# Residual sums by transposes in PSUM, the norm factor after the FFN products, and gate loads queued after weights

## The reference

```
h = rms_norm(x) ; p = h @ w_in
A = gated delta rule(p)   ; B = forgetting attention(p)
y = sigmoid(gA) * (A @ w_branch_a) + sigmoid(gB) * (B @ w_branch_b)
x = x + y @ w_out
x = x + (silu(n @ w_gate) * (n @ w_up)) @ w_down   with n = rms_norm(x)
out = rms_norm(x)         # each norm with its own gain vector
```

## Time and profile before

| what | us |
|---|---|
| device time, median of 3 runs | 1346.81 (1346.26 to 1347.42) |
| profiled execution, span first to last instruction | 1345.4 |
| PE busy | 1274.8 (95%) |
| DVE, ACT, POOL busy | 516.1, 470.4, 465.6 |
| mean granted TensorE clock | 0.971 of full |

### The profile page before, as it was taken

The page is one execution under the profiler, slowest core; times in us unless marked ns, Lnnn a source line. Parts: engine busy times, 40 slices in busy tenths (PEclk is TensorE's granted clock), DMA queues, the critical chain, the costliest instruction groups (busy, mean ns, idle before and its releaser), DMA issues.

```text
span 1345.4 us, 18394 instructions
## 1 busy us (share of the span) xinstructions
PE 1274.8 (95%) x6571; PEld 1062.1 (79%) x6571; DVE 516.1 (38%) x890; ACT 470.4 (35%) x890; POOL 465.6 (35%) x229
## 2 busy tenths in 40 slices
PE   5999979989899899999999998999799999999996
PEld 4868869879789798888888886878588888878884
DVE  4334452342342422466666674441333333330003
ACT  5344462433533523444444432323322222221113
POOL 5334440320411402333333322443344444444442
PEclk9999989998998999999999998999899999999998
DMA  6323320210211302433232206443133333332321
GB/s 168 81 71 94 99 73 25 71 48 24 80 44 44 94 25 70 118 89 87 87 87 86 86 16 217 134 118 94 36 104 95 94 94 95 103 115 85 92 73 63
DMA packets 172452, 113.66 MB, mean 84 GB/s; under 512 B 6257, under 2 KB 157922, under 8 KB 172402
## 3 DMA queue, kind: packets, MB, share of 16 engines
q1 hardware_dynamic: 166034, 98.26, 25.8%
q10 hardware_dynamic: 6368, 14.72, 3.0%
HBM read 104.54 MB, written 8.42 MB: 84 GB/s over the span
## 4 chain that ended last, share of the span: by engine, by line
PE 41%; issue 17%; POOL 5%; DVE 1%; ACT 1%; POOLq 0%; DVEq 0%; ACTq 0%
PE ps L1150 28%; PE ps L1494 9%; POOL w_lo L493 5%; PE ps L1238 2%; PE ps L1132 1%; POOL rstd L488 0%; DVE xn L1103 0%; ACT raw L564 0%; DVE Tm L946 0%; DVE h_lo L846 0%; DVE mixT L1124 0%; ACT tmp L803 0%; DVE Tm L949 0%; DVE L L944 0%; DVEq L64 0%
## 5 line engine op out<-in xcount | busy, mean ns | idle before, releaser
L493 POOL TENSOR_TENSOR w_lo<-raw,w_hi 128x1024 fp32r<-128x1024 f32 x170 | 415.4, 2444 | 791.9 <-ACT w_hi L554 791.9
L1150 PE MATMUL ps<-h_hi,w_lo 128*128 128x512 f32 x992 | 407.8, 411 | 0.0
L1150 PE MATMUL ps<-h_hi,w_hi 128*128 128x512 f32 x992 | 391.5, 395 | 4.7 <-DVE h_lo L846 2.6
L1150 PE MATMUL ps<-h_lo,w_hi 128*128 128x512 f32 x992 | 393.1, 396 | 0.0
L554 ACT ACTIVATE w_hi<-raw 128x1024 fp32r<-128x1024 f32 x170 | 180.4, 1061 | 577.3 <-PE ps L1150 480.4
L1150 PEld LDWEIGHTS ps<-h_lo,w_hi 128*128 128x128 f32 x992 | 187.1, 189 | 38.9 <-issue 1.0
L1150 PEld LDWEIGHTS ps<-h_hi,w_hi 128*128 128x128 f32 x992 | 187.9, 189 | 36.7 <-DVE h_lo L846 3.1
L1150 PEld LDWEIGHTS ps<-h_hi,w_lo 128*128 128x128 f32 x992 | 189.5, 191 | 32.0 <-issue 1.0
L867 DVE SCALAR_TENSOR_TENSOR tmp<-ps,prm,tmp 128x511 f32<-128x511 f32 (+2 forms) x72 | 53.9, 749 | 92.3 <-ACT tmp L591 87.1
L1113 DVE TENSOR_TENSOR tmp<-gate,ps 128x512 f32<-128x512 f32 x22 | 15.1, 688 | 154.1 <-PE ps L1150 154.1
L820 DVE TENSOR_TENSOR f_lo<-tmp,f_hi 128x512 f32 x22 | 58.9, 2675 | 2.7
(11 more groups left out here) (228 smaller groups left out, 1662.3 us busy)
## 6 DMA issues: line engine op xcount, KB each, us to landing
raw<-in_w_in SPq DMA_DIRECT2D x80, 512.0 KB, 3.9
raw<-in_w_gate SPq DMA_DIRECT2D x22, 512.0 KB, 3.8
raw<-in_w_up SPq DMA_DIRECT2D x22, 512.0 KB, 3.8
raw<-in_w_down SPq DMA_DIRECT2D x22, 512.0 KB, 3.8
gate_dram<-gate ACTq DMA_DIRECT2D x24, 256.0 KB, 2.0
cumb<-cum_dram ACTq DMA_DIRECT2D x8, 512.0 KB, 3.6
raw<-in_w_branch_a SPq DMA_DIRECT2D x8, 512.0 KB, 6.0
raw<-in_w_branch_b SPq DMA_DIRECT2D x8, 512.0 KB, 3.7
```

The source lines that it names most:

```text
L493: pool.tensor_tensor(w_lo[:, r % 2, :], raw[:, r, :], w_hi[:, r % 2, :], ALU.subtract)\
L1150: return pe.matmul(ps[:, bank, :], wts[wl][k], acts[xl][:, k, :], start=(n == 0), stop=(n == len(PASSES) - 1))
```

## The change

- **Layout.** `half_neg` becomes 32 floats, `prm` 128 floats, the small per-row tiles 32 floats each: all multiples of 128 bytes.
- **SP.** Weight loads of group i+1 are issued ahead of the gate loads of group i. ACT's `branches` is as before.
- **OUT.** PE adds the residual to the bank of the unit by four transposes without clearing (`residual`). ACT and DVE take `h_hi`, `h_lo` from the sum with the gain alone; DVE also copies it to `x2T`. PE turns `x2T` to token-major banks 4 to 7 only for the row sums.
- **FFN.** The factor is spread to a 128x512 tile `rstdb` by one matmul on a diagonal tile (`wide_row`). DVE multiplies both products by it, ACT applies Silu in place and makes `f_hi`.
- **Down.** f is stationary and the weights move, one k-tile to a load, so the sum is token-major. x2T is added by transposes during k = 1. The last k-tile goes row block by row block.

```diff
+    LINE = 32
-        half_neg = keep("half_neg", [P, 2 * H])
-        prm = keep("prm", [P, NPRM])
+        half_neg = keep("half_neg", [P, LINE])
+        prm = keep("prm", [P, P])
-        ss = keep("ss", [P, 2 * TT])
+        ss = keep("ss", [P, LINE])
...
@@ block.sync
-            with sp.Fori(0, KT // 2) as i:
+            def load_ab(i):
                 for r in range(4):
                     load(i + AB0, r, col_tile(w_branch_b if r >= 2 else w_branch_a,
                                               (i + AB0) * (2 * P) + (r % 2 - 2 * AB0) * P))
+            def load_gates(i):
                 for r in range(2):
-                    sp.wait_ge(b_low, led(b_low, FH // 2))
                     sp.wait_ge(y_sum, led(y_sum, i * 2 + r - 1))
                     sp.dma_start(gin[:, r, :, :], gate_dram[1:3, bass.ds(i * 2 + r, 1)]
                                  .rearrange("k j p n -> p (k j) n")).then_inc(gin_loaded[r], 16)
+            def load_out(i):
+                for r in range(4):
+                    load(i + OUT0, r, col_tile(w_out, i * (4 * P) + r * P))
+            load_ab(0)
+            load_ab(1)
+            sp.wait_ge(b_low, led(b_low, FH // 2))
+            load_gates(0)
+            with sp.Fori(1, KT // 2 - 1) as i:
+                load_ab(i + 1)
+                load_gates(i)
+            load_out(0)
+            load_gates(KT // 2 - 1)
+            load_out(1)
...
@@ block.gpsimd
+            for r in range(3):
+                low_part(FFN0, r)
+            pool.wait_ge(ms_ready, TT + 1)
+            power(rstd[:, 0:TT], ms[:, 0:TT], TT).then_inc(rstd_ready, 1)
+            low_part(FFN0, 3)
...
@@ block.scalar
+            def half_squares(a):
+                act.wait_ge(x2_turned, 4 * a + 4)
+                for t in range(TT):
+                    act.activation(gin[:, t // 2, t % 2, :], ps[:, 4 + t, :], ACT.Square,
+                                   accum_out=ss[:, a * TT + t:a * TT + t + 1]).then_inc(sq_summed, 1)
+            for j in range(KT):
+                high_ahead(OUT0 + j // 4, j % 4)
+                act.wait_ge(unit_done, OUT0 * 4 + j + 1)
+                act.activation(h_hi[:, j, :], ps[:, j % 4, :], ACT.Copy,
+                               scale=prm[:, NFFN + j:NFFN + j + 1]).then_inc(h_high, 1)
+                if j == 4:
+                    half_squares(0)
+            half_squares(1)
+            def ffn(i, first=False):
+                high_ahead(i + FFN0, 0)
+                if first:
+                    act.wait_ge(wide_done, 1)
+                    act.activation(rstdb[:, :], ps[:, 4, :], ACT.Copy).then_inc(wide_ready, 1)
+                silu(i, 0)
+                if not first:
+                    f_high(i - 1, 1)
+                high_ahead(i + FFN0, 1)
+                high_ahead(i + FFN0, 2)
+                silu(i, 1)
+                f_high(i, 0)
+                high_ahead(i + FFN0, 3)
...
+            for t in range(TT):
+                act.wait_ge(down_done, t + 1)
+                act.activation(raw[:, t, :], ps[:, 2 * t:2 * t + 2, :].rearrange("p b n -> p (b n)"),
+                               ACT.Square, accum_out=ss[:, 2 * TT + t:2 * TT + t + 1]).then_inc(sq_summed, 1)
@@ block.vector
+                    if kept:
+                        copy(x2T[:, k, :], ps[:, k % 4, :]).then_inc(x2_copied, 1)
...
+            def ffn_pair(i, k, first=False):
+                j = i * 2 + k
+                dve.wait_ge(unit_done, (i + FFN0) * 4 + 2 * k + 1)
+                dve.tensor_tensor(gate[:, k, :], ps[:, 2 * k, :], rstdb[:, :], ALU.mult)\
+                    .then_inc(ffn_scaled, 1)
+...
+                dve.wait_ge(unit_done, (i + FFN0) * 4 + 2 * k + 2)
+                dve.tensor_tensor(tmp[:, k, :], ps[:, 2 * k + 1, :], rstdb[:, :], ALU.mult)\
+                    .then_inc(ffn_up, 1)
+                dve.wait_ge(ffn_gate, led(ffn_gate, j + 1))
+                dve.tensor_tensor(tmp[:, k, :], tmp[:, k, :], gate[:, k, :], ALU.mult).then_inc(ffn_mul, 1)
...
@@ block.tensor
+            def x2_turn(j):
+                def go():
+                    pe.wait_ge(x2_copied, j + 1)
+                    if j == 4:
+                        pe.wait_ge(sq_summed, 2 * TT)
+                    for t in range(TT):
+                        last = turn(ps[:, 4 + t, j % 4 * P:(j % 4 + 1) * P], x2T[:, j, t * P:(t + 1) * P])
+                    last.then_inc(x2_turned, 1)
+                return go
+            for j in range(KT):
+                if j >= 4:
+                    pe.wait_ge(h_low, KT + j - 3)
+                    pe.wait_ge(x2_copied, j - 3)
+                unit(OUT0 + j // 4, j % 4, y_hi, y_lo, [x2_turn(j - 1), residual(j)] if j else [residual(j)],
+                     None if j else (y_low, led(y_low, KT)))
+            def ffn(i, first=False):
+                for r in range(4):
...
+                    tasks = ([x2_turn(KT - 1)], [], [wide_row], [])[r] if first else ()
+                    unit(i + FFN0, r, h_hi, h_lo, tasks, (h_low, 2 * KT) if first and r == 0 else None)
+            def down(k):
...
+                if k == FT - 1:
+                    order = [(t, n, p) for t in range(TT) for p in range(3) for n in range(2)]
+                else:
+                    order = [(t, n, p) for p in range(3) for t in (2, 3, 0, 1) for n in range(2)]
+                for at, (t, n, p) in enumerate(order):
...
+                    last = pe.matmul(ps[:, 2 * t + n, :], xt[:, k, t * P:(t + 1) * P],
+                                     wt[:, r % 2, n * 512:n * 512 + 512], start=(k == 0 and p == 0),
+                                     stop=(k == FT - 1 and p == 2))
```

More of the change, by code:

```diff
@@ L558, in high_ahead, with norm_high @@
                 high_part(q if r < 2 else q + 1, (r + 2) % 4)
[L560 to L567, removed]
+            def norm_high(col):
                 for k in range(KT):
-                    act.wait_ge(x_turned, KT * n + k + 1)
+                    act.wait_ge(x_turned, k + 1)
                     act.activation(h_hi[:, k, :], ps[:, k % 4, :], ACT.Copy,
@@ L779, in _ @@
-            act.wait_ge(out_added, led(out_added, KT))
-            half_squares(1, x_res, lambda t: xn2[:, t, D // 2:])
-            norm_high(1, NFFN)
-            def ffn(i):
-                for r in range(4):
-                    high_ahead(i + FFN0, r)
-                    if r % 2 == 0:
-                        act.wait_ge(unit_done, (i + FFN0) * 4 + r + 1)
-                        act.wait_ge(ffn_mul, led(ffn_mul, i * 2 + r // 2 - 1))
-                        act.activation(gate[:, r // 2, :], ps[:, r, :], ACT.Silu).then_inc(ffn_gate, 1)
@@ L1442, in _, with add_turned @@
                     unit(i + AB0, r, b_hi if r >= 2 else a_hi, b_lo if r >= 2 else a_lo)
-            def out_group(i):
-                def back_turn(r):
-                    def go():
-                        pe.wait_ge(out_taken, led(out_taken, i * 4 + r + 1))
-                        pe.wait_ge(out_added, led(out_added, i * 4 + r - 1))
-                        for t in range(TT):
-                            last = turn(ps[:, 4 + r % 2, t * P:(t + 1) * P], back[:, r % 2, t * P:(t + 1) * P])
-                        last.then_inc(out_turned, 1)
-                    return go
-                for r in range(4):
-                    pe.wait_ge(out_taken, led(out_taken, i * 4 + r - 3))
-                    unit(i + OUT0, r, y_hi, y_lo, [back_turn(r - 1)] if i or r else [],
-                         None if i or r else (y_low, led(y_low, KT)))
-                if i == KT // 4 - 1:
-                    back_turn(3)()
+            def add_turned(bank, col, src, stop=False):
+                return pe.matmul(ps[:, bank, col:col + P], src, ident[:, :], start=False, stop=stop,
+                                 is_transpose=True)
@@ new lines, in wide_row @@
+            def wide_row():
+                pe.wait_ge(diag_ready, 1)
+                pe.matmul(ps[:, 4, :], step[:, 4 * P:5 * P], tmp[:, 0, :], start=True, stop=True)\
+                    .then_inc(wide_done, 1)
+            def ffn(i, first=False):
+                for r in range(4):
+                    if not first:
+                        s = ffn_up if r % 2 else ffn_scaled
+                        pe.wait_ge(s, led(s, i * 2 + r // 2 - 1))
+                    tasks = ([x2_turn(KT - 1)], [], [wide_row], [])[r] if first else ()
+                    unit(i + FFN0, r, h_hi, h_lo, tasks, (h_low, 2 * KT) if first and r == 0 else None)
@@ L1475, in _ @@
             pe.wait_ge(h_low, 2 * KT - 1)
[L1476 removed]
+            pe.wait_ge(x2_copied, KT - 1)
+            ffn(0, True)
             with pe.Fori(1, FT // 2) as i:
                 ffn(i)
[L1481 to L1500 removed]
@@ L1516 @@
+            pe.wait_ge(ffn_scaled, led(ffn_scaled, FT))
+            pe.wait_ge(ffn_low, led(ffn_low, FT - 2))
+            for k in range(FT):
+                if k == FT - 2:
+                    pe.wait_ge(ffn_low, led(ffn_low, FT))
+                down(k)
```

272 lines of the change are left out of this document (121 added, 151 removed).

## The result

The changed kernel takes 1358.94 us (median of 4 runs, 1354.71 to 1359.85); beside it the kernel before took 1346.53 (4 runs). The ratio is 1.0089, interval 1.0072 to 1.0105: 0.9% slower, clear of noise. The forecast was 1353 with a range of 1340 to 1362, slower: direction and range held, the size was half of what came (+6.2 forecast; +12.4 between the medians, +12.7 between the two profiled spans, 1345.4 and 1358.1).

The account below looks back on a forecast made before the run. PE, busy for 95% of the span, was taken as the bound. Terms 20.3 - 4.3 + 8.0 - 7.1 - 0.95 - 2.3 - 7.4 = +6.2 took 1345.4 to 1351.6, with 1.4 for the median 1353; range 1340 to 1362.

Parts of the forecast that it names:

- AB: AB: gate loads behind weights make PE stand 4.5 us, plus 2.2 of half clock, for groups 1 to 3; +20.3 us.
- The 1.0 for `y_lo`: End of AB's group 3: late gate products on DVE let OUT begin some 1.0 us after the weights.
- OUT: OUT: PE stands 0.7 us ahead of the 12th matmul in seven units, more after the squares; +8.0 us, 56.4 against 48.4.
- OUT to FFN and FFN: OUT to FFN 9.9 us instead of 17.0, with a 5.9 stop (-7.1); FFN hides vector work, stop before down goes (-0.95).
- Layout: All stages: with lines of 128 bytes, matmuls moving 512 columns take 0.227 us everywhere; small matmuls in delta rule and attention -4.3.
- the forecast's own sign of being wrong: Wrong if sigmoids in groups 1 to 3 do not wait for DMA, or matmuls on a and y stay at 0.234.
- Start: Delta rule and attention, ahead of AB: 1216 + 320 small matmuls 3 ns cheaper each by layout; -4.3 us.
- Down and tail: Down 123.4 us against 125.7, -2.3; tail after the last matmul 7.7 us against 15.1, -7.4.
- Gates in time: Rival, AB: gates reach ACT by T1 + 6.7, no stops, AB -9.0 instead of +20.3, time 1324; chance 0.12.
- Full clock: Rival, AB and FFN: the four new stops leave the clock up, 8.8 us less, 1344; chance 0.14.
- The clock falls in OUT: Rival, OUT: standing and transposes drop the clock, 192 matmuls cost 40 us more, 1388; chance 0.03.
- FFN no longer hides: Rival, FFN: DVE holds POOL 2.7 us in each second unit, 15 us more, 1368; chance 0.05.

Follow-up runs that it names:

- experiment 1: The kernel before with only SP's new order, next group's weight loads ahead of the gate loads: 1366.01 us, 1.0152 of before.
- experiment 2: The changed kernel with SP's old order of loads in AB and OUT: 1338.82 us, 0.995 of the kernel before.
- experiment 7: Changed kernel, SP's old order, OUT's x2T turn ahead of the 16th matmul, ACT rounding in the first FFN group without waiting for the wide row: 1323.13 us, 0.985.
- experiment 9: On experiment 7: group 0's gates ahead of half of group 1's weights, its sigmoids later, and staged tiles a multiple of 2048 bytes from h_hi: 1312.52 us, 0.9768.
- 4: The kernel before with y_hi and y_lo lying in the place of h_hi and h_lo: 1339.79 us, one run, no interval.
- Experiment 3: The kernel before with only the small tiles' sizes changed, so every tile starts on a whole line of 128 bytes: 1343.32 us, 0.9984.
- experiment 5: The kernel before with h_hi and h_lo declared behind the small tiles: 1355.98 us, 1.0077.
- 11: On experiment 9: four small attention tiles moved behind b_lo, so a and b also start at a multiple of 2048 bytes: 1312.33 us, 0.9751.

## Why the prediction was right, and where its size was off

- **AB, +18.2 for +20.3: right in mechanism and place.** The last weight load at T1 + 3.6, the gates right behind it, rounding behind the sigmoids, POOL last: every link is in the timeline, and experiment 1 shows it alone. Each stop was 0.8 less than the 4.5 taken, because the three loads took 6.7 us (844.5 to 851.2) and not 7.5. The 1.0 for `y_lo` was too small: the stop ahead of OUT is 7.50, 3.8 more than the others, of which the forecast had 1.0. I had charged one operation stretched by POOL; it was two, since POOL ran two subtractions in a row. The half clock was booked in AB for all three stops (6.6); that behind the last one fell into OUT, and this alone makes AB some 2.4 too dear in the forecast and OUT as much too cheap.
- **OUT, +12.3 for +8.0: the stops right, the size 4.3 short.** Of it 2.4 came from outside, that half clock behind the 7.50 (experiment 2 against the changed kernel). The four turns behind a stop take 0.66 and not 0.44 (7 x 0.22 = 1.5). The matmul at 0.232 instead of 0.227 makes 192 x 0.005 = 1.0, and six stops of 0.61 instead of 0.7 take 0.5 off.
- **OUT to FFN and FFN, -8.9 for -8.05: right.** The stop was 5.78 for 5.9, and experiment 7 prices it with its clock at 7.4 (forecast 5.9 + 2.2 = 8.1). The 0.45 before unit 2 was 0.21. The FFN hides the vector work: this row of the changed kernel's groups (count, then busy us and mean ns of one, then idle time before them) has `f_lo` at 1.8 us each, under the 2.68 of before, and from OUT's end to down PE is idle for 6.0 of 248.7 us, which the two stops of 0.21 and 5.78 explain. The vector work itself was put too high, 6.8 us a pair; the new product of two SBUF tiles ran at 0.69 and not 2.7, so a pair takes 3 x 0.69 + 1.8 = 3.9.

```profile
L1130 DVE TENSOR_TENSOR f_lo<-tmp,f_hi 128x512 f32 (+1 forms) x22 | 39.5, 1794 | 33.8 <-ACT f_hi L801 33.8
```

- **Layout, the step that failed.** I read 33/32 off the ratio of 0.234 to 0.227, took a line of 128 bytes for enough, and let the moving tile alone decide. It took -2.3 from down (it was +0.7, and -2.1 with experiment 9), some 1 each from AB and OUT, and -4.3 for small matmuls. In down the third assumption fails by itself: its moving tiles lay well and it still ran at 0.232, because f, now stationary, lay 384 bytes off. By the forecast's own sign of being wrong (a and y staying at 0.234) this part was wrong: they came to 0.233 and 0.232. The small matmuls show nothing of it: their spacing moving a staged tile, 112 ns, and moving `ident`, 108 to 109, is the same in every layout; the 3 ns between 275 and 272 were between two kinds of matmul, not two places.
- **Start, -1.7 for -4.3: the clock's doing.** The first matmul on a falls between 788.1 and 796.1 in the kernels tried, with no order by layout. It goes roughly with the time that the clock records have at the half level ahead of it: 51.2 us in the kernel before (794.8), 47.8 in the changed one (793.1), 41.0 in experiments 7 and 9 (789.5, 790.6), 34.1 in 4 (788.1). Half of the difference is about what the start moved. Experiment 3 is 2 us off this (44.4, 793.8), experiment 5 has the dear h on top (41.0, 796.1). Why an execution gets more or fewer such spells is open.
- **Down and tail.** Tail -8.1 for -7.4: right. The 0.96 ahead of down is gone, as said.
- **Rivals.** "Gates in time" is out: ACT waited 31.9 us for them. "Full clock" is out: the granted clock over the last three groups is 0.91. "The clock falls in OUT" is out: with stops of 0.6 and transposes in every unit it is 1.00 (experiment 2). So the loss of clock that the rule of the Trainium skill would lead one to expect ("TensorE: Matmul & The Clock Gate", section "Part 4: PE-mode transpose": a transpose does not count as PE work in the same way) did not come. It is a weak test of the rule, since 5.6 us of each unit are matmuls. "FFN no longer hides" is out by the row above.

Measured less forecast, the misses are: start 2.6, AB -2.1, OUT 4.3, OUT to down -0.9, down 3.0, tail -0.7, together 6.2 of the 6.5 missing. The layout is behind 3.0 of down and 1.0 of OUT, and the 4.3 taken for the start had no ground; the clock and the longer turns are the rest of OUT. That AB came out 2.1 under and OUT 4.3 over is in good part the same 2.4 of half clock on the wrong side of the cut.

## What to carry to other kernels

When a load is moved behind others in a queue, follow its arrival into the in-order engine that consumes it: here ACT waited for the gates with the next weights' rounding queued behind, and PE stood 3.6 us for each group and more ahead of OUT. Such a stop costs its clock too (7.4 us for 5.8), and the best versions (experiments 9 and 11, 0.977 and 0.975) came from keeping the change's arithmetic, taking out such stops one by one, and then the layout. Place the tiles of a product, the stationary one as well as the moving one, by measuring the spacing of its matmuls, not by a ratio that fits a guess.

## What the runs showed of the hardware that I had not expected

- A matmul moving 512 columns of fp32r takes 0.227 us in the large products when both its tiles start at multiples of 256 bytes from `h_hi`, 0.232 to 0.234 with one of them 128 bytes off such a multiple, 0.233 to 0.2345 with it off a 64-byte boundary. It holds for the stationary tile as for the moving one (down, 0.232 and 0.227). How far back the tile lies does not matter.
- While POOL subtracts 128x1024, DVE's sum of two tiles in SBUF takes 2.47 instead of 0.69, and its rounding 2.34 instead of 0.43 (changed kernel, 911.94 and 916.56); POOL stays at 2.4 to 2.56 each. Two in a row on POOL catch two on DVE.
- After stops of 3.6 to 7.5 us the granted clock was at its half level for a while (AB 0.91, OUT 0.95); after stops of 0.6 in each unit of 7.3 it was not (1.00).
